# One masked copy per level: the recurrence matrix stored by chunk, with two copies handed to ScalarE

## The reference

```
b = cumsum(log f) over the steps of a chunk (per head and key channel d)
attn[t, s] = sum_d q[t, d] * k[s, d] * exp(b[t, d] - b[s, d])      for s <= t, else 0
o[t] = sum_s attn[t, s] * i[s] + (q[t] * exp(b[t])) @ state
state = exp(b_last) * state + sum_s (k[s] * exp(b_last - b[s])) (x) i[s]
o = rmsnorm(o) * norm_w, then * silu(g)
```

## Time and profile before

| what | value |
|---|---|
| median of three runs | 1179.83 us (1179.66 to 1180.95) |
| the profiled execution's own time | 1182.38 us |
| its span, first to last instruction | 1180.2 us |
| mean granted TensorE clock | 0.990 of full speed |
| TensorE busy | 1075.2 us, 91% |
| VectorE busy | 345.7 us, 29% |
| ScalarE busy | 213.7 us, 18% |
| GpSimd busy | 62.4 us, 5% |
| mean DMA rate | 372 GB/s |

### The profile page before, as it was taken

How to read it: one execution, slowest core, us unless ns; L and a number is a source line. 1 busy time by engine, 2 the same in 40 slices (tenths; PEclk the granted TensorE clock), 3 DMA queues, 4 the chain that set the end, 5 groups by cost and what they waited for, 6 DMA issues and landing times.

```text
span 1180.2 us, 13741 instructions
## 1 busy us (share of the span) xinstructions
PE 1075.2 (91%) x5571; PEld 518.0 (44%) x5571; DVE 345.7 (29%) x646; ACT 213.7 (18%) x338; POOL 62.4 (5%) x39
## 2 busy tenths in 40 slices
PE   7988999999999999998989898989898989898896
PEld 6867999643343434332323232323233323233332
DVE  4896648532211111111111111111111111111113
ACT  4632646300101111010101010101010101010102
POOL 0491003000000000000000000000000000000000
PEclk9998999999999999999999999999999999999999
DMA  8542556899999999999999999999999999999992
GB/s 280 212 144 72 194 186 215 287 385 401 395 428 427 426 429 428 428 428 430 428 428 428 428 430 428 428 428 429 429 428 429 428 429 428 428 428 429 427 425 117
DMA packets 46794, 438.88 MB, mean 372 GB/s; under 512 B 4852, under 2 KB 7176, under 8 KB 22184
## 3 DMA queue, kind: packets, MB, share of 16 engines
q1 hardware_dynamic: 44560, 435.99, 88.9%
q10 hardware_dynamic: 2200, 2.39, 0.6%
HBM read 437.32 MB, written 1.05 MB: 371 GB/s over the span
## 4 chain that ended last, share of the span: by engine, by line
PE 50%; DMA 42%; POOL 3%; DVE 3%; issue 1%; ACT 1%; DVEq 0%; SPq 0%; ACTq 0%; POOLq 0%
DMA S<-in_w_gate_up_dram 40%; PE PS L1476 17%; PE PS L1516 11%; PE PS L1247 7%; PE PS L1447 3%; PE PS L1455 2%; PE PS L1210 1%; DVE M L1106 1%; PE PS L1201 1%; POOL w_lo L352 1%; PE PS L1263 1%; POOL S L469 1%; DMA S<-in_w_in_dram 1%; POOL S L468 1%; PE PS L1266 1%
## 5 line engine op out<-in xcount | busy, mean ns | idle before, releaser
L1476 PE MATMUL PS<-S,M 128*64 128x512 f32 x2032 | 458.0, 596 | 45.1 <-DMA S<-in_w_gate_up_dram 44.4
L1476 PEld LDWEIGHTS PS<-S,M 128*64 128x64 f32 x2032 | 139.1, 137 | 343.0 <-issue 249.9
L1516 PE MATMUL PS<-S,M 128*64 128x512 f32 x1024 | 228.5, 599 | 27.5 <-DVE M L1106 27.5
L1092 DVE TENSOR_SCALAR M<-PS 128x256 f32<-128x256 f32 x64 | 27.0, 423 | 692.6 <-PE PS L1476 692.6
L1516 PEld LDWEIGHTS PS<-S,M 128*64 128x64 f32 x1024 | 71.1, 137 | 164.3 <-issue 129.2
L679 ACT ACTIVATE M<-M 128x256 f32<-128x256 f32 x64 | 26.7, 417 | 489.4 <-DVE M L1092 489.4
L684 ACT COPY M<-PS 64x512 f32<-64x512 f32 x32 | 18.5, 578 | 336.5 <-PE PS L1516 336.5
L1447 PE MATMUL PS<-M,XN 128*128 128x128 f32 x512 | 59.8, 275 | 0.0
L1447 PEld LDWEIGHTS PS<-M,XN 128*128 128x128 f32 x512 | 58.5, 192 | 0.5 <-issue 0.2
L1455 PE MATMUL PS<-M 128*128 128x512 f32 x120 | 55.5, 605 | 0.0
L352 DVE TENSOR_TENSOR w_lo<-S,hi_a 128x2048 fp32r<-128x2048 f32 (+1 forms) x20 | 42.2, 2127 | 6.1 <-ACT hi_a L514 6.0
(11 more groups left out here) (241 smaller groups left out, 829.9 us busy)
## 6 DMA issues: line engine op xcount, KB each, us to landing
S<-in_w_gate_up_dram SPq DMA_DIRECT2D x127, 2048.0 KB, 32.6
S<-in_w_down_dram SPq DMA_DIRECT2D x63, 2048.0 KB, 35.3
S<-in_w_in_dram SPq DMA_DIRECT2D x10, 2048.0 KB, 8.2
S<-in_w_out_dram SPq DMA_DIRECT2D x2, 2048.0 KB, 7.8
S<-in_w_in_dram SPq DMA_DIRECT2D x2, 1024.0 KB, 9.2
S<-in_moba_up_dram SPq DMA_DIRECT2D x1, 2048.0 KB, 7.7
S<-in_hgrn_up_dram SPq DMA_DIRECT2D x1, 2048.0 KB, 7.9
S<-in_w_down_dram SPq DMA_DIRECT2D x2, 1024.0 KB, 34.1
```

Of the source, the lines that this page charges most:

```text
L1092: v.tensor_scalar(gate[:, c], g2[:, :, 0], LIMIT, None, ALU.min).then_inc(gate_ready, 1)
L1476: ins = mm(gu[half][64 * g:64 * g + 64, :], hTe[:, k, tok], w, start=(k == 0), stop=(k == KD - 1))
L1516: ins = mm(multi[64 * n:64 * n + 64, :], actT[:, k, 64 * kh:64 * kh + 64], dn_slot[slot][:, k, 512 * n:512 * n + 512], start=(kh == 0 and ...
```

## The change

`AT` becomes p (g f t), with g = (b, h) and f the half of the columns. Its first half (f = 0) holds, for both halves of the partitions, the 64x64 block within the chunk (the same columns in all 128 partitions), so `take_level` is one masked copy of 128 partitions. Its second half (f = 1) holds level 6 in partitions 0 to 63. Level 6's products are now written for both blocks b to partitions 0 to 63, one bank wide, and ScalarE copies them in one instruction; ScalarE copies X too. As a block's upper 64 rows now have their columns elsewhere, the product with the values can't be one 128-row matmul: for each head and block a matmul of rows 0 to 63 writes 128 columns, then (X's product between them) one of rows 64 to 127 adds onto the upper 64 columns. A new semaphore, `o_upper`, makes TensorE wait for its own X product before the upper rows.

```diff
@@ bank_units
-    u += [("D", "dve"), ("X", "dve"), ("L6", "dve"), ("va0", "act"), ("L5", "dve"), ("L4", "dve"), ("va1", "act")]
+    u += [("D", "dve"), ("X", "act"), ("L6", "act"), ("va0", "act"), ("L5", "dve"), ("L4", "dve"), ("va1", "act")]
@@
-        AT = page(14).rearrange("p (b h t) -> p b h t", b=2, h=GH)
+        AT = page(14).rearrange("p (g f t) -> p g f t", g=2 * GH, f=2)
@@ scalar
             copy_out("ka1", kraw[:, 512:1024])
+            se.wait_ge(pool_ready, 2)
+            copy_out("X", CT.rearrange("p h t -> p (h t)"))
+            copy_out("L6", AT[0:CHUNK, :, 1, :], bank("L6")[0:CHUNK, :].rearrange("p (g t) -> p g t", t=CHUNK))
             decays(2)
@@ vector
             def take_level(name, m):
                 filled(ve, name)
-                for o in (0, CHUNK):
-                    r = slice(o, o + CHUNK)
-                    ins = v.copy_predicated(halves[r, :, r], MSK[r, m, :].unsqueeze(1).to_broadcast([CHUNK, 8, CHUNK]),
-                                            bank(name)[r, :].rearrange("p (b t) -> p b t", t=CHUNK))
-                drain(name, ins)
-                st.settle()
-            def take_level6():
...
+                drain(name, v.copy_predicated(AT[:, :, 0, :], MSK[:, m, :].unsqueeze(1).to_broadcast([P, 8, CHUNK]),
+                                              bank(name)[:].rearrange("p (g t) -> p g t", t=CHUNK)))
                 st.settle()
@@
             take_level("D", DIAG)
-            filled(ve, "X")
-            drain("X", v.tensor_copy(CT.rearrange("p h t -> p (h t)"), bank("X")[:]))
...
-                if LEVELS[n] == 6:
-                    take_level6()
-                else:
+                if LEVELS[n] != 6:
                     take_level(f"L{LEVELS[n]}", LEVELS[n])
@@ tensor, level
                         for b in range(2):
-                            ins = mm(ps[C * b:C * b + C, C * h:C * h + C], lhs[:, h, P * b:P * b + C],
+                            c = C * (GH * b + h)
+                            ins = mm(ps[0:C, c:c + C], lhs[:, h, P * b:P * b + C],
                                      rhs[:, h, P * b + C:P * b + P], start=True, stop=True)
@@ tensor, o0 and o1
-                for a in range(2):
-                    h = 2 * j + a
-                    c = slice(P * h, P * h + P)
-                    mm(ps[:, T * a:T * a + P], ib[:, 0, c], AT[:, 0, h, :], start=True, stop=True)
-                    mm(ps[:, T * a + P:T * a + T], ib[:, 1, c], AT[:, 1, h, :], start=True, stop=False)
-                    ins = mm(ps[:, T * a + P:T * a + T], ib[:, 0, c], CT[:, h, :], start=False, stop=True)
+                heads = [(T * a, 2 * j + a, slice(P * (2 * j + a), P * (2 * j + a) + P)) for a in range(2)]
+                for o, h, c in heads:
+                    for b in range(2):
+                        mm(ps[:, o + P * b:o + P * b + P], ib[0:CHUNK, b, c],
+                           AT[0:CHUNK, GH * b + h].rearrange("p f t -> p (f t)"), start=(o == 0 and b == 0), stop=True,
+                           skip_group_check=True)
+                for o, h, c in heads:
+                    ins = mm(ps[:, o + P:o + T], ib[:, 0, c], CT[:, h, :], start=False, stop=True, skip_group_check=True)
+                ins.then_inc(o_upper, 1)
+                pe.wait_ge(o_upper, j + 1)
+                for o, h, c in heads:
+                    for b in range(2):
+                        ins = mm(ps[:, o + P * b + CHUNK:o + P * b + P], ib[CHUNK:P, b, c],
+                                 AT[CHUNK:P, GH * b + h, 0, :], start=False, stop=True, skip_group_check=True)
```

More of the change, by code:

```diff
@@ L306, in hybrid_block @@
         ya_lo_ready, o_ready, o_hi_ready = sem("ya_lo_ready"), sem("o_ready"), sem("o_hi_ready")
+        o_upper = sem("o_upper")
         first_loaded, cst_loaded, router_loaded = sem("first_loaded"), sem("cst_loaded"), sem("router_loaded")
@@ L853, in cross_factors @@
                                        dec[:, 4:8].unsqueeze(2).to_broadcast([P, GH, C]), ALU.mult), kx_ready)
-            halves = AT.rearrange("p b h t -> p (b h) t")
             def take_level(name, m):
                 filled(ve, name)
-                for o in (0, CHUNK):
-                    r = slice(o, o + CHUNK)
-                    ins = v.copy_predicated(halves[r, :, r], MSK[r, m, :].unsqueeze(1).to_broadcast([CHUNK, 8, CHUNK]),
-                                            bank(name)[r, :].rearrange("p (b t) -> p b t", t=CHUNK))
-                drain(name, ins)
-                st.settle()
-            def take_level6():
[L870 to L874, removed]
+                drain(name, v.copy_predicated(AT[:, :, 0, :], MSK[:, m, :].unsqueeze(1).to_broadcast([P, 8, CHUNK]),
+                                              bank(name)[:].rearrange("p (g t) -> p g t", t=CHUNK)))
                 st.settle()
```

## The result

In ten runs each, the changed kernel took 1185.53 us (1182.97 to 1187.2) and the kernel before 1181.24 (1178.95 to 1183.35): a ratio of 1.0039, with a 95% interval of 1.0029 to 1.0049. By that ratio it is 4.6 us slower (3.4 to 5.8); the medians lie 4.3 apart. The profiled execution took 1185.1 us, with a span of 1183.3; before it was 1182.38 and 1180.2.

The account below looks back on a forecast made before the run. The DMA-bound expert weight stream waits on the first part, set by GpSimd's end and TensorE's work after it. 1.9 + 2.8 + 0 = 4.7 us on the median 1179.83 gave 1184.6 us, range 1181.2 to 1187.2.

Parts of the forecast that it names:

- What bounds the kernel: First part delays the DMA-bound expert weight stream; GpSimd's end and TensorE's work after 94 us count, VectorE savings alone nothing.
- Part 1: VectorE's fewer, wider copies up to the end of IB's low parts: GpSimd ends 1.9 us later, range 0 to 3.4.
- The three more turns: VectorE's turns of 0.57, 0.57 and 1.09 us ahead of GpSimd's end: 2.23 in all, less some 0.3.
- The price of 4.37: Replay's time in us for one GpSimd low part: half of 9.40, less one VectorE turn between.
- ScalarE's copies: Two copies of about 0.5 to 0.6 us each, free while ScalarE waits for level 4's differences.
- Level 6's matmuls: Eight matmuls, all to the array's lower column half: at worst 0.3 us before 64 us, covered by TensorE's wait.
- Part 2: o0 and o1 on TensorE: eight more matmuls, height changes and two waits add 2.8 us, range 1.2 to 3.9.
- going in: Switching TensorE from 128-row to 64-row passes costs 0.19 us, and again 0.19 going back.
- The gap of 0.3: Expected sign: TensorE idle 0.3 us before each L1355 group, from the new wait on `o_upper`, priced 0.31 each.
- Tiles in parallel: Different tiles run together: 0.34 us won at the o0 to o1 border, 0.5 more if the rule held fully.
- Part 3: Low clock after TensorE's wait for GpSimd: the same 2.6 us as before, so 0, with 1 us either way.
- The shift of the stream: Expert weight stream starts and ends 4.7 us later; rival that the delay is absorbed, 1179.8 to 1181: 8%.

Follow-up runs that it names:

- e6: The changed kernel with GpSimd forming IB's two low parts ahead of the rotary embedding of k's second half; ratio 0.9986 to the kernel before.
- e2: The kernel before with one masked copy per level and ScalarE copying X and level 6, o0 and o1 uncut; ratio 1.0014 to the kernel before.
- e7: The changed kernel with lower-row matmuls of o0 in turn with upper-row ones of o1, then the other halves; ratio 1.0027 to the kernel before.
- e3: The changed kernel with each masked copy done three times, giving VectorE 1.5 us more per level; ratio 1.0047 to the kernel before.
- e1: The kernel before, its layout kept, with only o0 and o1 cut into row halves with the two waits; ratio 1.0042 to the kernel before.
- e8: The changed kernel with IB's low parts formed sooner on GpSimd and o0 and o1's row halves in turn; 1176.95 us, ratio 0.9970 to the kernel before.
- e9: The changed kernel with 14 idle matmuls filling TensorE's pause before ib0's products to keep the clock up; ratio 1.0037 to the kernel before.

## Why the prediction was right

The forecast was 1184.6 against a median of before of 1179.83, a ratio of 1.0040; measured was 1.0039. By its steps:

- **What bounds the kernel: right.** A saving on VectorE shortened nothing in this order; GpSimd's end and TensorE's own work behind it counted. e6 shows it from the other side: with GpSimd's end 6.4 us earlier, G comes 6.4 earlier, and the runs are 6.3 shorter.
- **Part 1: 1.92 forecast, 1.79 measured**, in e2 the same alone. Level 1's factors were foreseen 26.6 and 27.8 us after R (82.5 and 83.7 in before's time) and came at 26.61 and 27.71. One detail was off. The three more turns were to lie all ahead of the rotary embedding's end, which was to come 1.92 later; it came only 0.80 later (29.50 after R, not 28.70), and the two low parts took 10.39 in place of 9.40. L828, level 0's differences, is why: it ended at 83.73, 1.08 behind the rotary embedding's end, and the two low parts with one turn of 0.57 between are just the 9.31 that are left to 93.04. So its turn of 1.09 fell on the other side of the border, and the sum stayed. The rule is this trace's own, the turns of the earlier trace rows. (The price of 4.37 for one of GpSimd's low parts doesn't follow from its working, as half of 9.40 less 0.57 is 4.42; but from L834's end at 89.63 to 93.99 it is 4.36.) The copy of 128 partitions takes 0.75, as taken from the earlier trace rows.
- **ScalarE's copies: right.** L507 takes 0.59 and 0.58 at 60.93 and 61.95, and ScalarE's exponentials wait for VectorE's differences behind it all the same. Level 6's matmuls took 1.15 us, 0.46 more than before and not at most 0.3; the wait of 13.1 covers them.
- **Part 2: 2.84 forecast, 2.75 measured.** The single prices can be read in the chain: eight passes of L1346 in 1.08 are 0.88 and 0.20 for going in; the product behind is 0.19 longer; at the border five of L1355 take 0.77 and the other three run beside those of o1, a gain of 0.33. The change into X's product and the wait behind it were priced at 0.19 + 0.31 = 0.50 for each of o0 and o1. The four passes of L1350 and the gap take 0.66 + 0.04, 0.26 over 4 x 0.11, and L1355's eight take 1.10, 0.22 over 0.88: together 0.48. The gap of 0.3 that was to be seen ahead of L1355 is thus no gap of its own but 0.04 and a longer group on either side.
- **Tiles in parallel.** The gain was at the border alone, where a lower and an upper group meet. With passes of lower and upper rows in turn (e7), it is 2.0 us, in which are also one wait and four changes of height fewer (two, where after has six). The Trainium skill's sentence that different tiles run in parallel (TensorEngine Tiling, section Key Properties) agrees with e7's 0.06 a pass; that the passes have to stand in turn for it is what after, with its eight in a row, adds. Whether it needs the two banks as well, no run shows.
- **Part 3: 0 forecast, -0.72 measured, inside the 1 us either way.** The clock was low again after a pause of 13.1, as after 7.6, but rose sooner after the return: that it would be low was right, its 2.6 us were not. Over all the profiles in which the pair follows GpSimd's wait at low clock, it took 5.35 to 6.80, with no order by the length of the wait (6.40 after 7.6 us, 5.53 after 6.7, 5.68 after 13.1); what decides it stays open.
- **The shift of the stream: right**, with a rest. G to the last product was 921.5 and 921.7 before, 922.6 and 922.0 after. Nothing was absorbed.

The terms on the chain give 3.82 us and the runs 4.6 (3.4 to 5.8), so the interval holds what the chain shows. The 0.8 between them is not settled, but it points behind G, which the sum put at nothing. The clock at the last product had its short form in all three profiles without either part of the change and its long form in both of after. The mean granted clock listed with the runs says how often a run is low: 0.988, as in both profiles of after, in seven of after's ten runs (1186.1 us on average, 1183.9 for the other three) and in 11 of the 72 of before that go with the experiments; for e2 it is 9 of 11, beside 1 of 17 of before on the same chip. So more low clock goes with the change; which stretch it is in a run without a profile, and why, stays open. The agreement of 1.0040 with 1.0039 is thus closer than its parts and in part luck: the clock's term was 0.7 too high, and something of that size behind G was not in the sum.

Two small slips of the working changed nothing: the chances named for "slower" come to 0.75 and not 0.77, and 7.5 above the median is 1187.3 and not 1187.2.

## What to carry to other kernels

Instructions saved on an engine that nobody waits for can lengthen the one that is waited for, if the two take turns and the saved ones took none: before shortening anything, ask what will then run beside what. Where such a saving costs something, first move the engine that is waited for out of the way (here GpSimd's low parts, 6 us), since after that the same saving may count for you. And of a matmul cut into halves of rows, order the halves of different banks in turn: cut in a row they took 5.24 us, in turn 3.23; uncut they had taken 2.68.

## What was not expected of the hardware

- More work on VectorE ended GpSimd's chain 2.0 us sooner (e3), since the added copies from PSUM took no turn from it and held back instructions that do.
- The granted clock fell to 0.50 while TensorE was busy, behind a stretch of 64-row matmuls with two short waits (e3, 170 to 172 us). In the same place the clock was 1.00 in the other profiles of the split form. It cost 1.36 us. Some 22 us behind G it fell in every profile, at the end of eight matmuls of 32 rows or just behind them, and in e1 while TensorE was busy without a gap. That the height of the matmuls is the cause, no run tests.
- A two-pass matmul of 64 rows in turn with one of the other 64 rows: a pass each 0.06 us on average, against 0.11 in a row (e7, e8).
- Keeping the clock up in the pause shortened the first part by 1.7 us in its profile, and the runs not at all (e9).
- The first part's stretches repeat within 0.05 us from one execution to the next, while its start is spread over 3 us, and from G to the last product it is 921.4 to 924.3 us. Of that spread, the five profiles with the longer stretch of low clock behind G have 922.7 to 924.3, the nine others 921.4 to 922.6. For a change of a few microseconds, the parts of the chain tell more than the spans.
